# Two of 336 expert weight units loaded through a source pattern whose outermost dimension is 8

## What is computed

```python
def swiglu(h, w_gate, w_up, w_down):
    return (jax.nn.silu(h @ w_gate) * (h @ w_up)) @ w_down
...
def moe_swiglu(h, w_router, w_gate, w_up, w_down):
    logits = (hf @ w_router).astype(jnp.float32)
    top_val, top_idx = lax.top_k(logits, TOP_K)
    gates = jax.nn.softmax(top_val, axis=-1)
    ...
    y = swiglu(hf[tok], w_gate[e], w_up[e], w_down[e])
    return y * gate[:, None].astype(y.dtype)
```

## Time and profile before

| | us |
|---|---|
| median of 3 runs | 1356.21 (1355.82 to 1356.37) |
| the profiled execution, its time | 1358.75 |
| the profiled execution, its span | 1357.0 |
| TensorE busy | 1314.3 (97%) |
| VectorE, ScalarE, GpSimd busy | 427.5, 305.1, 80.2 |
| granted TensorE clock, mean | 0.997 |

### The profile page before, as it was taken

One profiled execution on the slowest core, in us unless ns is written; L12 is line 12 of the kernel. 1 busy time (PEld: TensorE's weight loads), 2 busy tenths in 40 slices (PEclk: granted clock), 3 DMA queues, 4 the chain that ended last, 5 costly groups with the idle time before them and its releaser, 6 DMA issues.

```text
span 1357.0 us, 31023 instructions
## 1 busy us (share of the span) xinstructions
PE 1314.3 (97%) x13973; PEld 941.6 (69%) x13973; DVE 427.5 (32%) x719; ACT 305.1 (22%) x467; POOL 80.2 (6%) x76
## 2 busy tenths in 40 slices
PE   7999999999999999999999999999989999999985
PEld 7999999878888886665556666665546666665543
DVE  6987878965444560000000000000000000000002
ACT  5455455554444460000000000000000000000002
POOL 1511111010000000000000000000000000000000
PEclk9999999999999999999999999999999999999998
DMA  9644454357665578999999999999999999999993
GB/s 355 250 166 151 147 187 184 128 180 280 248 245 218 182 284 358 372 386 403 419 412 419 417 421 406 420 418 406 419 421 412 419 418 405 421 418 418 408 420 152
DMA packets 68425, 447.45 MB, mean 330 GB/s; under 512 B 7920, under 2 KB 10608, under 8 KB 16192
## 3 DMA queue, kind: packets, MB, share of 16 engines
q1 hardware_dynamic: 63456, 436.57, 80.1%
q0 software_dynamic: 4400, 8.30, 2.3%
q10 hardware_dynamic: 432, 0.54, 0.1%
HBM read 438.70 MB, written 6.68 MB: 328 GB/s over the span
## 4 chain that ended last, share of the span: by engine, by line
PE 89%; DMA 5%; SPq 4%; ACT 1%; DVE 1%; issue 1%; ACTq 0%; DVEq 0%
PE bank L1783 37%; PE bank L1802 14%; PE bank L444 10%; PE bank L446 10%; PE bank L445 10%; SPq L465 3%; DMA raw_late<-in_expert_units 2%; DMA w_raw<-in_expert_units 2%; PE bank L1730 2%; PE bank L1546 1%; PE bank L1528 1%; PE bank L1561 1%; PE bank L1762 1%; DMA qkT<-in_xT 1%; PE bank L1536 0%
## 5 line engine op out<-in xcount | busy, mean ns | idle before, releaser
L400 DVE TENSOR_TENSOR w_lo<-raw,w_hi 128x2048 fp32r<-128x2048 f32 x70 | 160.5, 2293 | 60.6 <-ACT w_hi L395 60.4
L395 ACT ACTIVATE w_hi<-raw 128x2048 fp32r<-128x2048 f32 x71 | 135.9, 1914 | 90.1 <-PE bank L446 84.1
L444 PE MATMUL bank<-w_hi,a_hi 128*128 128x256 f32 (+1 forms) x400 | 136.5, 341 | 1.0 <-DVE a_lo L1154 0.5
L446 PE MATMUL bank<-w_hi,a_lo 128*128 128x256 f32 (+1 forms) x400 | 133.9, 335 | 0.0
L445 PE MATMUL bank<-w_lo,a_hi 128*128 128x256 f32 (+1 forms) x400 | 133.9, 335 | 0.0
L1280 DVE TENSOR_TENSOR h<-sg,bank 128x384 f32<-128x384 f32 (+1 forms) x56 | 28.2, 504 | 301.8 <-PE bank L1802 163.1
L1286 DVE COPY hT_x<-bank 128x128 f32<-128x128 f32 x35 | 10.1, 290 | 352.3 <-ACT hT_x L842 352.3
L444 PE MATMUL bank<-a_hi,w_hi 128*128 128x256 f32 x384 | 112.4, 293 | 8.6 <-DVE w_lo L982 8.6
L446 PE MATMUL bank<-a_hi,w_lo 128*128 128x256 f32 x384 | 110.2, 287 | 0.0
L445 PE MATMUL bank<-a_lo,w_hi 128*128 128x256 f32 x384 | 110.2, 287 | 0.0
L842 ACT ACTIVATE hT_x<-bank 128x256 f32<-128x256 f32 x35 | 13.4, 383 | 420.1 <-PE bank L1730 420.1
(11 more groups left out here) (302 smaller groups left out, 1861.0 us busy)
## 6 DMA issues: line engine op xcount, KB each, us to landing
w_raw<-in_expert_units SPq DMA_DIRECT2D x86, 1024.0 KB, 28.1
raw<-in_units SPq DMA_DIRECT2D x71, 1024.0 KB, 4.9
raw<-in_expert_units SPq DMA_DIRECT2D x60, 1024.0 KB, 27.6
raw_more<-in_expert_units SPq DMA_DIRECT2D x45, 1024.0 KB, 27.4
raw_late<-in_expert_units SPq DMA_DIRECT2D x45, 1024.0 KB, 27.6
extra<-in_expert_units SPq DMA_DIRECT2D x30, 1024.0 KB, 26.9
a_raw<-in_expert_units SPq DMA_DIRECT2D x28, 1024.0 KB, 26.5
aside_raw<-in_expert_units SPq DMA_DIRECT2D x15, 1024.0 KB, 27.5
```

The lines of the kernel that those rows point to most:

```text
L395: nc.scalar.activation(w_hi[:, u % SPLIT, :], where, ACT.Copy).then_inc(hi_ready, 1)
L400: nc.vector.tensor_tensor(w_lo[:, u % SPLIT, :], home(u)[0], w_hi[:, u % SPLIT, :].bitcast(F32), ALU.subtract).then_inc(lo_ready, 1)
L444: nc.tensor.matmul(bank, hi, w[0], start=start, stop=False)
L446: return nc.tensor.matmul(bank, lo, w[0], start=False, stop=stop)
```

## The change

The host makes a second copy of two units, for all experts: unit 150 and unit 250 (`BY_EIGHT`), with the 128 partition rows reordered. Row p = 16 b + a of the unit stands at place 8 a + b of the copy. The load of these two units reads the copy with the pattern b, a, n: 8 outermost, then 16, then 8 KB rows. Rows therefore land in the same partitions as before. The destination is the same buffer and is written as a plain 128 x 2048 block. The number of transfers, the bytes, the semaphores, the waits and the order on SP stay as they are; 334 units are loaded as before.

```diff
+BY_EIGHT = (150, 250)
...
+            def load_by_eight(m, e, home):
+                where, landed, _value = home
+                sp.dma_start(where, interleaved[m, bass.ds(e, 1)].rearrange("o (a b) n -> (o b) a n", b=8)).then_inc(landed, 16)
...
-                load(expert_source(j, e), expert_home(i, j))
+                if n in BY_EIGHT:
+                    load_by_eight(BY_EIGHT.index(n), e, expert_home(i, j))
+                else:
+                    load(expert_source(j, e), expert_home(i, j))
...
+    arrays["interleaved"] = np.stack([packed_experts[n % UE].reshape(E, 8, P // 8, UNIT).transpose(0, 2, 1, 3).reshape(E, P, UNIT)
+                                      for n in BY_EIGHT])
```

More of the change, by code:

```diff
@@ L171, with program @@
 SCATTER = ((0, 0, 7), (1, 0, 3), (0, 1, 6), (1, 1, 5))
-def program(nc, x_in, xT_in, pool_scale, router, final_norm, units, expert_units, mask_in, cos_in, sin_in, ident_in, iota_in,
+def program(nc, x_in, xT_in, pool_scale, router, final_norm, units, expert_units, interleaved, mask_in, cos_in, sin_in, ident_in, iota_in,
             upto_in, poolmat_in, inv_count_in, token_in,
```

## The result

The median before is 1356.29 us (1355.82 to 1356.78, 4 runs), after it is 1381.38 us (1380.99 to 1382.11, 4 runs). The ratio is 1.0184, with a 95% interval from 1.0172 to 1.0196: 25.1 us slower. The forecast was 1351.2 us and the range ended at 1361.6. The profiled execution of after took 1382.11 us, 1380.3 of them its span; before's span is 1357.0.

The account below looks back on a forecast made before the run. The prediction took the last weight transfer's landing, on eight late DMA engines, to bound the end; relieving them by 5.0 us, with issue and cover at 0, gave 1356.21 - 5.0 = 1351.2 us, range 1350.4 to 1361.6.

Parts of the forecast that it names:

- What bounds the kernel: Wide experts set by TensorE, narrow ones by transfers; the last unit's landing at 1340.74 us sets the end.
- Two sets of eight, 12.8 us apart: At the end, eight DMA engines finish at 1326.3 us on average, the other eight at 1339.1.
- that relief: At the end, late engines spared 2 x 2.50 = 5.0 us over the two units, giving a 5.0 us gain.
- the instruction packets: Candidate for the late engines' gap: 112 packets, 109 us of engine time, 13.6 us each on eight engines.
- SP's issue at no cost: On SP, two replaced issues cost 0; even doubled issues, +2 us each, would be hidden.
- The cut over eight, +2.50 us on each: At units 150 and 250, eight engines carry 128 KB each, +2.50 us per unit; the others 2.50 less.
- Which eight: Early eight taking both units gives 1351.2 us, chance 0.45; late eight gives 1361.2, chance 0.27.
- the late eight: Rival: the late engines get both units, end 5.0 us later, time 1361.2 us; chance 0.27.
- Cover for the two units, "I take 0": At units 150 and 250, 37.7 and 35.7 us from issue to read cover the +2.5 us; cost 0.
- The rival of the shared way: Shared partition access slows late engines by the 64 KB spared: 2.50 us given and taken back, 1356.2 us; chance 0.20.
- The sign that I named for it: At units 150 and 250, the rate would show a dip only if engines share a way.
- The range: Whole-kernel time 1350.4 to 1361.6 us, reaching to the slower late-eight case; likeliest case alone 1350.4 to 1352.6.

Follow-up runs that it names:

- the cuts over sixteen: Units 150 and 250 read from the reordered copy with outermost dimension 16 in place of 8, against the kernel before: 1369.52 us, ratio 1.0099.
- the halves: Units 150 and 250 loaded from the original array in two transfers of 64 partitions each, against the kernel before: 1369.70 us, ratio 1.0111.
- the pair on its own partitions: Units 150 and 250 loaded only in partitions 0 to 7 and 32 to 39, by two engines, against the kernel before: 1350.21 us, one run.
- unit 60: Only one unit loaded by eight, unit 60 in place of unit 150, against the kernel before: 1365.11 us, ratio 1.0065.
- the dense stage: Units 6, 7 and 8 there by eight, by sixteen and in partition halves; 150 and 250 as before; against the kernel before: 1355.74 us, one run.
- The transfers with 2 and 4: Outermost dimension 4 or 2: unit 150 whole by four, 1364.35 us; units 150 and 250 partly, four or two engines crossing, 1357.75 and 1355.02 us; against the kernel before.

## Why the prediction was wrong

*What bounds the kernel.* Right: the last landing set the end. But I called the wide experts TensorE's and didn't draw the consequence of the DMA share of 1.01 in the same windows. From 600 us on the transfers never catch up with anything, so each us lost there arrives at the end. In after 8.5 us are lost at unit 150 while TensorE loses 0.2 us in the same window, and with unit 150 alone by eight the end, 500 us later, is 11.5 us late: the 8.5 are still owed.

*Two sets of eight, 12.8 us apart.* Borne out. In before the sixteen reports for the last unit come in two groups, eight from 1324.6 to 1329.0 us and eight from 1337.3 to 1340.7, and their means are 12.8 us apart. Both the cuts over sixteen and the halves kept the plateau. And the run with the pair on its own partitions relieves every late engine by 5.0 us and gains 4.4, in one run: nearly the size that the forecast gave to that relief. That kernel leaves most of two units out, so it shows the worth of the relief and not a way to it. That the instruction packets make the gap was not tested and stays a candidate.

*SP's issue at no cost.* Right: 6.0 us and 2.2 us for the two, where usual ones took 2.6 to 2.7 each; the 3 us more at unit 150 are hidden, as SP stayed some 27 us ahead.

*The cut over eight, +2.50 us on each.* Right: 16 packets fewer, and eight reports for the unit.

*Which eight.* Wrong in a way that no case foresaw. It was neither the early nor the late eight but six early ones and two late. This mixture is as bad as the late eight, since the end asks for the slowest engine: +5.0 us for those two, the plateau of two engines at the end of after. Even without the larger loss the forecast of 1351.2 would have missed, with a time of about 1361, just inside the range.

*Cover for the two units, "I take 0".* The step that failed most: by the windows 19.3 of the 25.1 us come from here, and the sum had them at nothing. I priced the longer transfer by whether TensorE would wait for this unit. That was nearly right: there was no wait at unit 150, and at unit 250 TensorE waited 0.6 us for it, at 1141.5. The 1.5 us before that, at 1134.8, and the 1.1 us after it, at 1143.8, end with matmuls of other units. What I didn't price was what the transfer does to the queue it stands in. Timeline of TensorE in after around unit 250 (start us, us, what, then the idle time before and what ended it):

```profile
1134.78 0.41 PE L1812 MATMUL bank<-w_raw,hT_x 128*32 128x256 f32 x2 [1.50 <-issue]
...
1141.54 1.07 PE L1812 MATMUL bank<-a_raw,hT_x 128*32 128x256 f32 x16 [0.56 <-DMA a_raw<-in_interleaved]
1143.75 1.07 PE L1812 MATMUL bank<-w_raw,hT_x 128*32 128x256 f32 x16 [1.14 <-DMA w_raw<-in_expert_units]
```

*The rival of the shared way, 1356.2.* The right mechanism with the wrong sum. I let an early engine slow only the late one whose partitions it writes, and by just the 64 KB that this one was spared, so that it came to nothing. Measured: as soon as two engines cross, all sixteen fall to half rate, for as long as the crossing lasts. For unit 150 that is 128 KB at half rate, 10 us, for the early engines and 10 us again for the two late ones, 20 us at half rate or 10 lost; the windows say 8.5. The sign that I named for it, a dip of the rate at units 150 and 250, was the right one to look for, and it was the first thing to be seen. With the correct price the case gives 1356.3 + 19.3 + 5.0 = 1380.6.

*The range.* Its slow end, 1361.6, held only the engines' own bytes. The cost of two engines on one set of partitions stood nowhere in the trace of before, and I bounded it by assuming that it would stay with these two. A bound from both sides would have let all of them pay, as a resource shared by all would make them: half rate for 10 us or more a unit, 10 us of loss in all at the least, with an end at 1366 or beyond.

Nothing that ran beats the kernel before on the full work. By these prices I don't see it done with crossing transfers: two engines at a time cost all sixteen half their rate, and one alone takes from the owner what it spares him.

## What to carry to other kernels

In a stream that keeps all DMA engines busy, a transfer has to be priced by what it does to the rate of the whole queue, not by whether its own data come in time: look at GB/s beside the DMA share, since here the share stayed near 1.01 while the rate halved. Keep the cut of a transfer into SBUF so that each engine writes the partitions it always writes (128 rows; halves of columns were free, halves of partitions cost 7 us for each MiB). The divisors tried here, 2, 4, 8 and 16, cost roughly in proportion to how long two or more engines were at it; others were not tried. Where engines end at different times, moving bytes off the last ones can help only if none of them is among the receivers, as two of them were here.

## What was not expected of the hardware

- One engine on another's partitions slows two engines (360 to 406 GB/s of 419), two slow all sixteen (197 to 246), four and eight do the same (188 to 254). Why the step is so sharp is open: the records carry no engine numbers, and two sharing partitions explain only four slow engines.
- With all eight at it at the same time and usual units behind them it is deeper than half, 147 to 184 GB/s at unit 60 and 147 to 172 in the dense stage. The packets then take 0.79 us in the median at unit 60 and 0.91 in the dense stage, towards three times 0.31; by the rule of the swizzle two crossing engines and the owner stand on the same partitions of the upper half there. Whether that is the reason was not tested.
- The engines that a transfer by eight takes are not one of the two sets that end 12.8 us apart, but six of one and two of the other. The transfers with 2 and 4 fit with early engines alone.
- A transfer by eight that crosses is slow with nothing else in the queue too: 120 GB/s with a DMA share of 0.58, so 12.9 GB/s for each busy engine in the place of 26.2.
